# The first norm of a two-layer backbone: row-wise modulation in a block of its own, or tiles turned unscaled and modulated by feature inside the modulation's block

## The chip, the core and the metric

The kernel runs on one NeuronCore of one Trainium2 chip. Everything is one launch, and the metric is the device time of that launch in microseconds. All data are float32. The core's engines are TensorE (PE, with its weight loads PEld), VectorE (DVE), ScalarE (ACT), GpSimd (POOL) and the queues; SP only issues DMAs. Each engine runs its own program in order and waits on semaphores.

## What is computed

A diffusion backbone of two layers over 256 context tokens and 512 latent tokens, 1024 features each. Each layer normalises and modulates its input, mixes tokens by two kinds of attention or a gated linear scan, and then sends each token through 128 experts picked from 16384. The part that matters here is the very beginning of layer 0:

```python
def rmsnorm(x, g):
    y = x * lax.rsqrt(jnp.mean(x * x, axis=-1, keepdims=True) + EPS)
    return y * g

def modulate(h, shift, scale):
    return h * (1 + scale) + shift

def modulation(cvec, w_mod, b_mod):            # w_mod: (1024, 6 * 1024)
    m = jax.nn.silu(cvec) @ w_mod + b_mod
    return jnp.split(m, 6, axis=-1)

mx = modulation(c, w_mod[i], b_mod[i])         # latent stream
mc = modulation(c_ctx, w_mod[i], b_mod[i])     # context stream
hx = modulate(rmsnorm(x, norm1[i]), mx[0], mx[1])
hc = modulate(rmsnorm(h, norm1[i]), mc[0], mc[1])
ox, oc = mix_even(hx, hc, e_w_in[j], ...)      # begins with h @ w_in, w_in: (1024, 2304)
```

So for each of the two streams there is one shift and one scale vector of 1024 features, and the normed input is `x / rms(x) * gain * (1 + scale) + shift`. The gain times (1 + scale), and the shift, depend on the feature alone; 1 / rms depends on the token alone.

## The kernel before

Tokens lie on partitions in six tiles of 128 (`NT` = 6; tiles 0 and 1, `CT` = 2, are context, 2 to 5 are latent) in the SBUF tensor `R` (128 x 6 x 1024). A matmul against the 1024 features wants the features on partitions, so the normed tiles are turned by TensorE (a transpose is a matmul against the identity `ident`) into `hT` (128 x 8 x 768: feature within a block of 128, block `k` of `KC` = 8, token).

The program is a row of blocks (`nc.Block()`): in each, every engine gets its own list, and all engines meet at its end. The end of a block, together with the clearing of the semaphores of its stage on SP, is a barrier. The blocks at the start of the launch are these:

1. `start` (stage "mod", lines 183 to 252). SP loads `c` and `c_ctx`, then eight pieces of `w_mod` of 1 MB each (line 140), for columns 0 to 2047 of the modulation: shift and scale of the first norm. The ring `w` has eight places (`Modulation(m, a, s, 0, [0], KC, (0, 1))`). ACT computes an exponential for silu (line 205), and then issues all the other loads on its own queue: six small ones (lines 207 to 209), the band mask (210), `R` in two transfers of 1 and 2 MB (211, 212), `ident` (213), `iota` (214). PE multiplies each piece as it lands (line 159: four matmuls per piece, a stationary operand of two columns, one per stream, in four column groups of the array). DVE adds the bias (line 170, four instructions, into `row`: four groups of two partitions, at partitions 0, 32, 64, 96, 512 columns each). POOL stores these rows to the DRAM tensor `modulations` (line 178). ACT ends its list with a wait for all of its loads.
2. `modulated_norm` (stage "n00", lines 275 to 333). SP reads the gain and the four modulation rows back from DRAM, each spread over 128 partitions (lines 269, 272: `NormVectors.load`), and then prefetches the first two fifths of the projection's weights (line 359, four transfers of 1 MB). ACT takes the sum of squares of each tile (296) and a root (298). DVE makes gain * (1 + scale) for both streams (310), a reciprocal (315), and for each tile `R * (1/rms) * scale` (319) and `+ shift` (322). PE turns the tile (331, eight transposes of 128 x 128, two PSUM banks), ACT copies it to `hT` (302). Two pairs of PSUM banks alternate.
3. `project_heads` (stage "ph0", line 365 on). PE runs 30 units (`units`, line 430): 5 column blocks `n` by 6 tiles `t`, each of eight matmuls over `k` (shown as 16 by the trace), with `hT[:, k, t * P:(t + 1) * P]` as the stationary operand, into four PSUM banks. ACT squares a unit's result (445), DVE sums (475), scales and rotates it. DVE first waits for the tables of gains, cosines and sines (`tables_loaded`), which SP issues at the block's beginning (lines 410, 412). From unit 10 on, pieces of the modulation's later columns are slipped in between the units.

After that come the attention of the context, the experts of layer 0, layer 1 and its experts. The experts take most of the launch; they gather 8 KB rows of two tables from HBM.

## Time and profile before

| | us |
|---|---|
| three runs of the kernel before | 4306.64, 4318.24, 4319.30 |
| their median | 4318.24 |
| the profiled execution's own time | 4310.87 |
| its span, from first to last instruction | 4309.5 |
| blocks `start` and `modulated_norm`: start of the launch to the first matmul of the projection | 69.9 |

In the rows further down, times are microseconds from the start of the span, and a matmul of the program may be counted as two instructions. A row of the timeline gives the start, the length, the engine (PEld is TensorE's weight load; SPq, ACTq and DVEq are the instruction queues of these engines, where DMAs are issued), the line, the operation, output <- input, and how many instructions are merged in the row; in brackets stands the idle time of that engine ahead of it and what ended it. `PEclk` is the granted clock of TensorE as a share of 2.4 GHz.

### The profile page before, as it was taken

The numbers are of one execution on the slowest core, as the hardware profiler recorded it, in microseconds if no ns is written. First come the engines' busy times: TensorE is split into PE (matmuls) and PEld (weight loads), VectorE is DVE, ScalarE is ACT, GpSimd is POOL, SyncE is SP. The second block draws the span as 40 slices with busy tenths as digits, with TensorE's granted clock in tenths as the row PEclk, the third lists the DMA queues.
The fourth block names the chain that finished last, engine by engine and source line by source line (L and its number), as shares of the span: only waits on it lengthen the run. The fifth ranks groups of instructions, "written<-read, shape, count | busy, mean of one in ns | idle before, by whom it ended". The sixth has DMA issues, their size and how long they took to land. (4 is left out here: it accounts for less than half of the span.)

```text
span 4309.5 us, 44681 instructions
## 1 busy us (share of the span) xinstructions
PE 3738.7 (87%) x12806; PEld 1933.6 (45%) x12806; DVE 2605.5 (60%) x5677; ACT 1754.8 (41%) x5153; POOL 1700.3 (39%) x1349
## 2 busy tenths in 40 slices
PE   5998798899999899978898978788999997787877
PEld 2345644555554445423444436556444552222222
DVE  2534787667865855687654445437876458766544
ACT  1123355555554443433333334323663333333333
POOL 0100244444444444445444432002444435556665
PEclk9999999999999999999999999899999999999999
DMA  4354899999999999999999983028999999999998
GB/s 178 148 225 178 328 422 408 402 421 422 397 421 426 425 419 425 427 391 427 427 427 427 427 360 111 1 106 321 421 413 426 424 423 403 427 427 427 427 427 359
DMA packets 245901, 1561.98 MB, mean 362 GB/s; under 512 B 30995, under 2 KB 41267, under 8 KB 74518
## 3 DMA queue, kind: packets, MB, share of 16 engines
q0 software_dynamic: 185088, 1342.36, 74.5%
q1 hardware_dynamic: 56998, 211.95, 13.0%
q10 hardware_dynamic: 3568, 4.81, 0.3%
q8 instruction: 102, 1.67, 0.1%
q14 instruction: 145, 1.19, 0.1%
HBM read 1550.65 MB, written 8.36 MB: 362 GB/s over the span
## 5 line engine op out<-in xcount | busy, mean ns | idle before, releaser
L2898 PE MATMUL ps<-ring,ex_diag 128*128 128x512 f32 x5120 | 2474.1, 618 | 408.2 <-ACT ex_diag L2887 380.1
L1657 POOL DMA_INDIRECT ring<-in_p_uv,expert x1280 | 1643.9, 1284 | 2146.9 <-PE ps L2898 1417.1
L2862 DVE SCALAR_TENSOR_TENSOR ring<-ring,H 128x1024 f32<-128x1024 f32 x1280 | 1558.1, 1224 | 1085.4 <-DMA ring<-in_p_uv,expert 1059.9
L2898 PEld LDWEIGHTS ps<-ring,ex_diag 128*128 128x128 f32 x5120 | 924.7, 194 | 1644.7 <-ACT ex_diag L2887 819.5
L2881 ACT ACTIVATE ex_act_w<-ex_dots 128x1 f32<-128x1 f32 x1280 | 257.9, 201 | 1463.3 <-DVE ring L2862 1454.0
L2887 ACT ACTIVATE ex_diag<-ident_sb,ex_weight 128x128 f32<-128x128 f32 x1280 | 514.0, 402 | 93.0 <-issue 4.7
L2883 ACT ACTIVATE ex_weight<-ex_act_w,gates 128x1 f32<-128x1 f32 x1280 | 377.1, 295 | 90.8 <-issue 3.5
L430 PE MATMUL ps<-win_w,hT 128*128 128x512 f32 (+1 forms) x480 | 191.9, 557 | 1.6 <-PEq L283 1.4
L430 PEld LDWEIGHTS ps<-win_w,hT 128*128 128x128 f32 x480 | 90.4, 191 | 104.4 <-issue 102.1
L2020 PEld LDWEIGHTS ps<-hTc,bs_w 128*128 128x128 f32 x768 | 110.8, 191 | 29.3 <-issue 23.5
L2020 PE MATMUL ps<-hTc,bs_w 128*128 128x128 f32 (+1 forms) x768 | 120.3, 310 | 0.3 <-issue 0.3
L2862 DVE DVE_READ_ACCUMULATOR ring<-ring,H 128x1 f32 x1280 | 104.7, 82 | 0.0
L2881 ACT ACT_TABLE_LOAD x72 | 92.4, 1283 | 1.9 <-issue 0.3
L445 ACT ACTIVATE ph_sq<-ps 128x512 f32<-128x512 f32 (+1 forms) x24 | 12.4, 517 | 164.9 <-PE ps L430 164.9
L475 DVE TENSOR_REDUCE ph_ss<-ph_sq 128x8 f32<-128x512 f32 (+1 forms) x24 | 14.1, 585 | 100.3 <-ACT ph_sq L445 100.3
L664 PEld LDWEIGHTS ps<-KV,bs_probsT 128*128 128x128 f32 x480 | 63.1, 192 | 24.4 <-issue 24.4
L751 ACT COPY bs_probsT<-ps 128x512 f32<-128x512 f32 (+1 forms) x72 | 36.8, 511 | 84.2 <-PE ps L676 73.9
L735 DVE TENSOR_REDUCE bs_top<-ps 128x2 f32<-128x1536 f32 (+2 forms) x32 | 49.8, 1557 | 33.8 <-PE ps L688 32.4
L2165 PEld LDWEIGHTS ps<-bs_w,hTc 128*128 128x128 f32 x512 | 60.9, 192 | 11.5 <-issue 11.5
L2020 PE MATMUL ps<-K,bs_w 128*128 128x256 f32 x256 | 65.7, 379 | 0.0
L1813 ACT COPY fc_qT<-ps 128x128 f32<-128x128 f32 x64 | 17.0, 265 | 115.1 <-PE ps L1770 111.2
L664 PE MATMUL ps<-KV,bs_probsT 128*128 128x64 f32 (+1 forms) x480 | 63.2, 271 | 0.1
(478 smaller groups left out, 3392.1 us busy)
## 6 DMA issues: line engine op xcount, KB each, us to landing
bs_w<-in_p_wqk SPq DMA_DIRECT2D x64, 576.0 KB
ring<-in_p_wqk SPq DMA_DIRECT2D x48, 576.0 KB, 4.9
ca_mod_w<-in_w_mod SPq DMA_DIRECT2D x24, 1024.0 KB, 12.8
ring<-in_p_uv,expert POOLq DMA_INDIRECT x1280
win_mod_w<-in_w_mod SPq DMA_DIRECT2D x16, 1024.0 KB, 4.9
bs_w<-in_e_w_out_tiles SPq DMA_DIRECT2D x24, 512.0 KB
win_w<-in_e_w_in SPq DMA_DIRECT2D x9, 1024.0 KB, 10.0
fc_w_q<-in_p_wqk SPq DMA_DIRECT2D x16, 576.0 KB
```

The source lines that it names most:

```text
L430: mm = pe.matmul(m.ps[:, u % 4, 0:halves * 256], m.hT[:, k, t * P:(t + 1) * P], pre.w[:, n % 2, 0:halves, k, :], start=(k == 0), stop=(k = ...
L664: mm = pe.matmul(self.O[:, cols], self.probsT[:, r % 2, x * P:(x + 1) * P], KV[:, self.blocks(n)[j], vals], start=(j == 0), stop=(j == las ...
L735: dve.tensor_reduce(self.top[:, n % 2, :], self.S[:, :, 0:w], AX.X, ALU.max)
L751: act.copy(self.probsT[:, r % 2, 0:wide], self.T[:, 0:wide]).then_inc(self.copied, 1)
L1657: pool.indirect_dma_start(m.ring[:, r, :], None, a["p_uv"], bass.IndirectOffsetOnAxis(ap=m.expert[:, t % 2, slot % SLOTS:slot % SLOTS + 1] ...
L2020: mm = pe.matmul(m.ps[:, self.q_banks[u % nq], 0:cols], w[:, j * P:(j + 1) * P], self.turned_of(self.tiles_of(u), j), start=(j == 0), stop ...
L2165: mm = pe.matmul(m.ps[:, 7, at:at + P], self.hT[:, k, i * P:(i + 1) * P], w[:, k * P:(k + 1) * P], start=(k == 0), stop=(k == KC - 1), ski ...
L2862: dve.scalar_tensor_tensor(out=ring[:, r, 0:D], in0=ring[:, r, 0:D], scalar=1.0, in1=h_of(t + t0), op0=ALU.mult, op1=ALU.mult, accum_out=d ...
L2881: act.activation(act_w[:, b:b + 1], dots[:, t % 2, n:n + 1], ACT.Gelu)
L2883: act.activation(weight[:, b:b + 1], act_w[:, b:b + 1], ACT.Copy, scale=gates[:, t % 2, n:n + 1])
L2887: act.activation(diag[:, b, :], m.ident[:, :], ACT.Copy, scale=weight[:, b:b + 1]).then_inc(diag_ready, 1)
L2898: mm = pe.matmul(mix_banks(t)[:, half, :], diag[:, b, :], ring[:, r, D + half * BANK:D + (half + 1) * BANK], start=(n == 0), stop=(n == SL ...
```

## The change

`start` takes over the whole norm, and `modulated_norm` and `NormVectors` are gone, with the block they made.

- ACT issues the two transfers of `R` and `ident` first, ahead of the exponential for silu, and the small ones behind it, with one new one: the gain by feature (`norm1_features`, 128 x 8, the eight feature blocks of each partition), laid out on the host.
- ACT then waits for `R` and `ident`, squares the six tiles, takes the root; DVE multiplies each tile by 1/rms alone (`Hn`, tensor_scalar); PE turns the tiles, ACT copies them unmodulated to `hT`.
- The ring of `w_mod` pieces has four places in place of eight. On PE, tiles 0 to 3 are turned between and behind the last four pieces, tiles 4 and 5 at the end.
- The modulation rows no longer go to DRAM and back. PE turns them from `row` with sixteen transposes of two partitions into 128 x 2 columns each; DVE copies these from PSUM (`feature`) and makes `h_shift` and `h_scale` (128 x 8 x 2: feature, block, stream). A multiply and an add with one scalar per partition (`modulate`) then treat `hT` in place, eight instructions for a stream: the context's inside the block, the latent's at the beginning of `project_heads` on DVE, where PE waits for it (`latent_ready`) ahead of unit 2.
- SP issues the prefetch of the projection's weights behind the last piece of `w_mod`.
- `eps` is set at the beginning.

```diff
     with Stage(nc, "mod") as s:
...
-        mods = Modulation(m, a, s, 0, [0], KC, (0, 1))
+        mods = Modulation(m, a, s, 0, [0], 4, (0, 1))
...
             @block.sync
             def _(sp):
...
                 mods.sync(sp)
+                pre.prefetch(sp)
 
             @block.scalar
             def _(act):
+                act.dma_start(m.R[:, 0:CT, :], a["ctx"].rearrange("b (t p) d -> p (b t) d", p=P)).then_inc(tiles_loaded, 16)
+                act.dma_start(m.R[:, CT:NT, :], a["x"].rearrange("b (t p) d -> p (b t) d", p=P)).then_inc(tiles_loaded, 16)
+                act.dma_start(m.ident[:, :], a["ident"]).then_inc(tiles_loaded, 16)
                 act.wait_ge(c_loaded, 32)
                 act.activation(den[:, :, :], craw[:, :, :], ACT.Exp, scale=-1.0).then_inc(exp_done, 1)
+                act.dma_start(gain[:, :], a["norm1_features"]).then_inc(gain_loaded, 16)
...
                 act.dma_start(m.iota[:, :], rows(a["iota"])).then_inc(streams_loaded, 16)
+                act.wait_ge(tiles_loaded, 48)
+                act.wait_ge(eps_ready, 1)
+                for t in range(NT):
+                    act.activation(Hn[:, t, :], m.R[:, t, :], ACT.Square, accum_out=ss[:, t:t + 1])
+                    act.drain()
+                act.activation(ss[:, :], ss[:, :], ACT.Sqrt, bias=m.eps[:, :], scale=1.0 / D).then_inc(rms_ready, 1)
+                for t in range(NT):
+                    act.wait_ge(turned, t + 1)
+                    act.copy(m.hT[:, :, t * P:(t + 1) * P],
+                             m.ps[:, 2 + 2 * (t % 2):4 + 2 * (t % 2), :].rearrange("p b (k c) -> p (b k) c", c=P)).then_inc(copied, 1)
...
             @block.tensor
             def _(pe):
+                def turn(t):
+                    pe.wait_ge(h_ready, t + 1)
+                    if t >= 2:
+                        pe.wait_ge(copied, t - 1)
+                    for k in range(KC):
+                        tr = pe.transpose(m.ps[:, 2 + 2 * (t % 2) + k // 4, (k % 4) * P:(k % 4 + 1) * P],
+                                          Hn[:, t, k * P:(k + 1) * P], m.ident[:, :])
+                    tr.then_inc(turned, 1)
+
                 pe.wait_ge(silu_done, 1)
                 for n in range(mods.pieces):
                     mods.tensor(pe, n)
+                    if n >= mods.pieces - 4:
+                        turn(n - mods.pieces + 4)
+                for t in range(4, NT):
+                    turn(t)
+                pe.wait_ge(mods.row_ready, mods.COLS)
+                for n in range(ROWS):
+                    part, at = slice(32 * (n // 4), 32 * (n // 4) + 2), n % 4 * P
+                    tr = pe.transpose(m.ps[:, ROW_BANKS[n // 4], n % 4 * 2:n % 4 * 2 + 2], mods.row[part, 0, at:at + P], m.ident[part, part])
+                    if n % 4 == 3:
+                        tr.then_inc(rows_turned, 1)
...
                 dve.tensor_tensor(m.csil[:, :, 2:4].rearrange("p k s -> p s k"), craw[:, :, :], den[:, :, :],
                                   ALU.mult).then_inc(silu_done, 1)
+                dve.wait_ge(rms_ready, 1)
+                dve.reciprocal(ss[:, :], ss[:, :])
+                dve.drain()
+                for t in range(NT):
+                    dve.tensor_scalar(Hn[:, t, :], m.R[:, t, :], ss[:, t:t + 1], None, ALU.mult).then_inc(h_ready, 1)
                 mods.vector(dve, 0)
...
+                for j, bank in enumerate(ROW_BANKS):
+                    dve.wait_ge(rows_turned, j + 1)
+                    dve.tensor_copy(feature[:, 4 * j:4 * j + 4, :], m.ps[:, bank, 0:8].rearrange("p (n s) -> p n s", s=2))
+                dve.drain()
+                dve.wait_ge(gain_loaded, 16)
+                dve.tensor_copy(m.h_shift[:, :, :], feature[:, 0:KC, :])
+                dve.scalar_tensor_tensor(out=m.h_scale[:, :, :], in0=feature[:, KC:ROWS, :], scalar=1.0,
+                                         in1=gain[:, :].unsqueeze(2).broadcast_to([P, KC, 2]), op0=ALU.add, op1=ALU.mult)
+                dve.drain()
+                dve.wait_ge(copied, NT)
+                modulate(dve, m, 1)
                 dve.wait_ge(lam_exp_done, 1)
...
-            @block.gpsimd
-            def _(pool):
-                mods.store(pool)
...
+def modulate(dve, m, stream):
+
+    cols = slice(0, CT * P) if stream else slice(CT * P, TOK)
+    for k in range(KC):
+        done = dve.tensor_scalar(m.hT[:, k, cols], m.hT[:, k, cols], m.h_scale[:, k, stream:stream + 1],
+                                 m.h_shift[:, k, stream:stream + 1], ALU.mult, ALU.add)
+    return done
...
                     if t == 0:
                         pe.wait_ge(pre.loaded[n % 2], 16 * (2 * (n // 2) + halves))
+                    if u == CT:
+                        pe.wait_ge(latent_ready, 1)
...
+                modulate(dve, m, 0).then_inc(latent_ready, 1)
                 dve.wait_ge(tables_loaded, 96)
```

How the order moves on three engines. First TensorE, from the start of the launch, before (L159 the pieces of the modulation, L331 the turning of tiles, L430 the projection):

```order
L219 UNCONDITIONAL_BRANCH
L159 MATMUL ps<-mod_mod_w,csil 2x512 x32
L195 UNCONDITIONAL_BRANCH
L324 UNCONDITIONAL_BRANCH
L331 MATMUL ps<-ident_sb,Hn 128x128 x48
L283 UNCONDITIONAL_BRANCH
L421 UNCONDITIONAL_BRANCH
L430 MATMUL ps<-win_w,hT 128x512 x88
```

and TensorE now (L242 turns the tiles, L256 the modulation rows, L408 is the projection):

```order
L159 MATMUL ps<-mod_mod_w,csil 2x512 x20
L242 MATMUL ps<-ident_sb,Hn 128x128 x8
L159 MATMUL ps<-mod_mod_w,csil 2x512 x4
L242 MATMUL ps<-ident_sb,Hn 128x128 x8
L159 MATMUL ps<-mod_mod_w,csil 2x512 x4
L242 MATMUL ps<-ident_sb,Hn 128x128 x8
L159 MATMUL ps<-mod_mod_w,csil 2x512 x4
L242 MATMUL ps<-ident_sb,Hn 128x128 x24
L256 MATMUL ps<-ident_sb,mod_mod_row 128x2 x16
L199 UNCONDITIONAL_BRANCH
L397 UNCONDITIONAL_BRANCH
L408 MATMUL ps<-win_w,hT 128x512 x88
```

The turning has moved in between the pieces, so that pieces 5 to 7 stand behind the turning of tiles 0 to 2; one pair of branches (the end of a block) is gone.

Next ScalarE's queue at the start of the launch, before:

```order
L205 ACTIVATE mod_den<-mod_craw 128x16
L207 DMA mod_v<-in_a_lq 128x64
...
L208 DMA sink<-in_b_sink 128x8
L209 DMA gain_gn<-in_a_gn 128x128
L210 DMA band_sb<-in_band 128x2x128
L211 DMA R<-in_ctx 128x2x1024
L212 DMA R<-in_x 128x4x1024
L213 DMA ident_sb<-in_ident 128x128
L214 DMA iota_sb<-in_iota 128x16
```

and now:

```order
L209 DMA R<-in_ctx 128x2x1024
L210 DMA R<-in_x 128x4x1024
L211 DMA ident_sb<-in_ident 128x128
L213 ACT_TABLE_LOAD
L213 ACTIVATE mod_den<-mod_craw 128x16
L214 DMA mod_gain<-in_norm_features 128x8
...
L219 DMA band_sb<-in_band 128x2x128
L220 DMA iota_sb<-in_iota 128x16
L224 ACTIVATE Hn,mod_ss<-R 128x1024 x6
L226 ACT_TABLE_LOAD
L226 ACTIVATE mod_ss<-mod_ss,eps 128x6
```

The large transfers are now first on the queue, and the squares stand behind nine further issues on the same engine.

Last VectorE, behind silu, now (L275 is the multiply by 1/rms, L306 the modulation by feature; before, L319 and L322 stood here for each tile, in the second block):

```order
L272 RECIPROCAL mod_ss<-mod_ss 128x6
L275 TENSOR_SCALAR Hn<-R,mod_ss 128x1024 x6
L170 TENSOR_TENSOR mod_mod_row<-ps,mod_mod_bias 2x512 x4
...
L287 COPY mod_feature<-ps 128x8 x4
L290 COPY h_shift<-mod_feature 128x16
L291 SCALAR_TENSOR_TENSOR h_scale<-mod_feature,mod_gain 128x16
L306 TENSOR_SCALAR hT<-hT,h_scale,h_shift 128x256 x8
L298 SCALAR_TENSOR_TENSOR neg_lam<-mod_dots 128x1
L199 UNCONDITIONAL_BRANCH
L447 UNCONDITIONAL_BRANCH
L306 TENSOR_SCALAR hT<-hT,h_scale,h_shift 128x512 x8
```

The bias of the modulation (L170) stands behind the six multiplies, and behind it stands the chain that now ends the block.

## Rows read from the trace of the kernel before

**Rows 1.** Timeline of the first block, 0 to 36 us, all engines.
```profile
3.08 0.22 ACT L205 ACTIVATE mod_den<-mod_craw 128x16 f32<-128x16 f32 x1 [1.06 <-DMA mod_craw<-in_c_ctx]
...
4.96 0.45 ACTq L208 DMA_DIRECT2D sink<-in_b_sink  x1
5.45 1.32 ACTq L209 DMA_DIRECT2D gain_gn<-in_a_gn  x1
...
9.03 0.53 ACTq L212 DMA_DIRECT2D R<-in_x  x1
9.59 12.33 ACTq L213 DMA_DIRECT2D ident_sb<-in_ident  x1
...
21.95 2.31 ACTq L214 DMA_DIRECT2D iota_sb<-in_iota  x1
...
25.70 1.89 PE L159 MATMUL ps<-mod_mod_w,csil 128*2 128x512 f32 x8 [0.79 <-DMA mod_mod_w<-in_w_mod]
...
28.46 1.89 PE L159 MATMUL ps<-mod_mod_w,csil 128*2 128x512 f32 x8 [0.88 <-DMA mod_mod_w<-in_w_mod]
30.42 2.84 DVE L170 TENSOR_TENSOR mod_mod_row<-ps,mod_mod_bias 2x512 f32<-2x512 f32 x4 [26.32 <-PE ps L159]
```
**Rows 2.** Timeline of the second block, 36 to 70 us.
```profile
38.05 1.06 ACT L296 ACTIVATE Hn<-R 128x1024 f32<-128x1024 f32 x1 [3.79 <-PEq L195]
...
46.63 0.30 ACT L298 ACTIVATE n_ss<-n_ss,eps 128x6 f32<-128x6 f32 x1
49.60 2.36 DVE L310 SCALAR_TENSOR_TENSOR v_scale<-v_scale,v_gain 128x1024 f32<-128x1024 f32 x2 [15.15 <-DMA v_shift<-modulations]
52.08 0.19 DVE L315 RECIPROCAL n_ss<-n_ss 128x6 f32<-128x6 f32 x1
52.36 1.28 DVE L319 SCALAR_TENSOR_TENSOR Hn<-R,n_ss,v_scale 128x1024 f32<-128x1024 f32 x1
53.73 1.23 DVE L322 TENSOR_TENSOR Hn<-Hn,v_shift 128x1024 f32<-128x1024 f32 x1
...
55.01 1.97 PE L331 MATMUL ps<-ident_sb,Hn 128*128 128x128 f32 x8 [24.65 <-DVE Hn L322]
...
57.50 1.97 PE L331 MATMUL ps<-ident_sb,Hn 128*128 128x128 f32 x8 [0.53 <-DVE Hn L322]
...
67.48 1.09 PE L331 MATMUL ps<-ident_sb,Hn 128*128 128x128 f32 x8 [0.77 <-DVE Hn L322]
68.61 1.01 ACT L302 COPY hT<-ps 128x1024 f32<-128x1024 f32 x1 [0.85 <-PE ps L331]
```
**Rows 3.** Timeline, the projection's first work on each engine.
```profile
69.93 43.04 PE L430 MATMUL ps<-win_w,hT 128*128 128x512 f32 x96 [1.36 <-PEq L283]
...
72.56 0.51 SPq L412 DMA_DIRECT2D ph_sin<-in_rope_ab_sin  x1
...
78.67 0.60 ACT L445 ACTIVATE ph_sq<-ps 128x512 f32<-128x512 f32 x1 [9.05 <-PE ps L430]
...
85.54 0.60 ACT L445 ACTIVATE ph_sq<-ps 128x512 f32<-128x512 f32 x1 [6.27 <-PE ps L430]
```
**Rows 4.** Transfers issued from 0 to 120 us: count, size, us to landing.
```profile
R<-in_x ACTq DMA_DIRECT2D x1, 2048.0 KB, 25.6
...
gain_gn<-in_a_gn ACTq DMA_DIRECT2D x1, 64.0 KB, 18.9
...
ph_sin<-in_rope_ab_sin SPq DMA_DIRECT2D x1, 128.0 KB, 4.2
...
sink<-in_b_sink ACTq DMA_DIRECT2D x1, 4.0 KB, 16.7
```
**Rows 5.** Queues from 22 to 24 us: packets, MB, share; q1 is SP's, q10 ACT's.
```profile
DMA packets 213, 0.84 MB, mean 422 GB/s; under 512 B 19, under 2 KB 116, under 8 KB 116
...
q10 hardware_dynamic: 107, 0.05, 8.5%
q1 hardware_dynamic: 106, 0.79, 93.9%
```
**Rows 6.** The same from 26 to 28 us, where SP's pieces end.
```profile
q10 hardware_dynamic: 206, 0.57, 71.7%
q1 hardware_dynamic: 40, 0.22, 26.5%
```
**Rows 7.** TensorE's instructions of line 159, by tensor: min/median/max ns.
```profile
L159 PE MATMUL ps<-win_mod_w,csil x128: 589/592/592, 147.7 to 262.4; 128*2 128x512 f32 x128
...
L159 PE MATMUL ps<-mod_mod_w,csil x64: 1012/1036/1061, 6.8 to 29.3; 128*2 128x512 f32 x64
```
**Rows 8.** A warm group of line 159, and one of eight transposes, in the timeline.
```profile
155.94 1.04 PE L159 MATMUL ps<-win_mod_w,csil 128*2 128x512 f32 x8
...
411.41 1.04 PE L1759 MATMUL ps<-ident_sb,H 128*128 128x128 f32 x8
```
**Rows 9.** TensorE by stretch, 380 to 384 us: length, PE busy (instructions), PEclk, DMA share, GB/s.
```profile
380.00:381.00 1.00, 0.36 (x2) 0.50 0.98 356
381.00:382.00 1.00, 1.00 (x7) 0.50 1.04 414
382.00:383.00 1.00, 1.00 (x6) 0.50 0.86 270
383.00:384.00 1.00, 1.00 (x8) 0.61 0.96 365
```
**Rows 10.** The same by stretch, where the projection begins.
```profile
69.00:70.00 1.00, 0.07 (x1) 0.87 0.00 0
70.00:71.00 1.00, 1.00 (x2) 0.50 0.00 0
...
73.00:74.00 1.00, 1.00 (x3) 0.92 0.10 25
```
**Rows 11.** Groups by line and shape, VectorE: count, busy us, mean ns of one.
```profile
L720 DVE TENSOR_SCALAR bs_probs<-bs_probs,bs_rec 128x768 f32<-128x768 f32 x16 | 10.0, 624 | 0.0
...
L720 DVE TENSOR_SCALAR ca_probs<-ca_probs,ca_rec 128x256 f32<-128x256 f32 x8 | 2.8, 344 | 0.0
```
**Rows 12.** Timeline: eight matmuls with two moving columns, the nearest to the rows' turning.
```profile
2693.73 1.37 PE L1418 MATMUL ps<-lu_tri,LG 128*128 128x2 f32 x8
```

More of the change, by code:

```diff
@@ L180, in store, with start @@
             queue.wait_ge(self.stored[q], 16 * self.COLS * ((len(self.groups) - q + 1) // 2))
-def start(nc, m, a):
+def start(nc, m, a, pre, Hn):
+    ROWS, ROW_BANKS = 2 * KC, (6, 7, 0, 1)
     with Stage(nc, "mod") as s:
@@ L190, in start @@
         c_loaded, exp_done, silu_done = s.sem("c_loaded"), s.sem("exp_done"), s.sem("silu_done")
-        mods = Modulation(m, a, s, 0, [0], KC, (0, 1))
+        mods = Modulation(m, a, s, 0, [0], 4, (0, 1))
         v, junk, dots = s.sb("v", [P, 4, A_DQK]), s.sb("junk", [P, 2, A_DQK]), s.sb("dots", [P, 2])
-        v_loaded, streams_loaded = s.sem("v_loaded"), s.sem("streams_loaded")
-        dots_ready, lam_exp_done = s.sem("dots_ready"), s.sem("lam_exp_done")
+        ss, gain, feature = s.sb("ss", [P, NT]), s.sb("gain", [P, KC]), s.sb("feature", [P, ROWS, 2])
+        v_loaded, streams_loaded, tiles_loaded, gain_loaded = (s.sem(x) for x in ("v_loaded", "streams_loaded", "tiles_loaded", "gain_loaded"))
+        dots_ready, lam_exp_done, eps_ready = s.sem("dots_ready"), s.sem("lam_exp_done"), s.sem("eps_ready")
+        rms_ready, h_ready, turned, copied, rows_turned = (s.sem(x) for x in ("rms_ready", "h_ready", "turned", "copied", "rows_turned"))
         with nc.Block() as block:
@@ L227, in _ @@
                 dve.memset(m.csil[:, :, :], 0.0)
+                dve.memset(m.eps[:, :], EPS).then_inc(eps_ready, 1)
                 dve.wait_ge(exp_done, 1)
@@ L2956, in program @@
         CTILES, XTILES = range(CT), range(CT, NT)
-        m.h0 = 0
-        start(nc, m, a)
+        m.h_shift, m.h_scale = (ctx.enter_context(nc.sbuf_tensor(x, [P, KC, 2], F32)) for x in ("h_shift", "h_scale"))
         def later_scores(layer):
@@ L2962, in later_scores @@
             return both.rearrange("p t d -> p (t d)").rearrange("p (h k) -> p h k", k=NK)
+        m.h0 = 0
         m.later_scores = later_scores
@@ L2967, in program @@
             with nc.sbuf_tensor("hT0", [P, KC, TOK], F32) as m.hT:
-                with nc.sbuf_tensor("Hn", [P, NT, D], F32) as Hn, Stage(nc, "win0") as s:
-                    pre, mods = InWeights(m, a, s), Modulation(m, a, s, 0, [1, 2], 2, (4, 5))
-                    with Stage(nc, "v00") as sv:
-                        vec = NormVectors(m, a, sv, 0, 0, "norm1", (0, 1))
-                        def prefetch(sp):
-                            vec.load(sp)
-                            pre.prefetch(sp)
-                        modulated_norm(nc, m, "n00", vec, range(NT), lambda t: Hn[:, t, :], prefetch)
-                    project_heads(nc, m, a, pre, mods)
+                with Stage(nc, "win0") as s:
+                    pre = InWeights(m, a, s)
+                    with nc.sbuf_tensor("Hn", [P, NT, D], F32) as Hn:
+                        start(nc, m, a, pre, Hn)
+                    with Stage(nc, "win0m") as sm:
+                        project_heads(nc, m, a, pre, Modulation(m, a, sm, 0, [1, 2], 2, (4, 5)))
                 context_attention(nc, m, a)
```

75 lines of the change are left out of this document (3 added, 72 removed).

## The prediction

> **What bounds the kernel now.** The change touches only the launch's first 70 us, so I read the timeline of that stretch first, then the DMA queues by stretch, and last the clock of TensorE. Blocks are barriers, so each has its own bound.
>
> In the first block the bound is the loads. TensorE's last piece of the modulation begins at 28.46 and is over at 30.4; VectorE's bias is done at 33.3 [rows 1], and `R`, issued at 9.03 and landing 25.6 us later [rows 4], comes at 34.6. The second block starts at 38.05 (its first square), and there a chain runs that no engine fills: the modulation rows come back from DRAM, and VectorE waits 15.15 us for them, until 49.60; then scale rows (2.36), reciprocal, and per tile 1.28 + 1.23 us of VectorE, a new tile every 2.5 us; the first tile is turned at 55.01, the last at 67.48, the last copy ends at 69.62 [rows 2]. The projection's first matmul is at 69.93 [rows 3]. From there on TensorE works without gaps: one unit takes 6.87 us (85.54 - 78.67 [rows 3]). So whatever the start of the projection gains should reach the end, and nothing else in the launch is touched. The sum is therefore one question: when does the projection start, instead of at 69.93?
>
> **The change part by part.**
>
> (a) The trip through DRAM, one barrier and the second source of VectorE's work go. Gone are 12 instructions of about 1.25 us and the two of 2.36 us together on VectorE [rows 2], and the waits around them. Nothing of that is on the new path; what is late instead is worked out step by step.
>
> (b) When `R` is there. From the start ACT's queue and SP's share the 16 DMA engines. In rows 5 they moved 106 and 107 packets in the same 2 us, though in bytes 0.79 against 0.05 MB: the engines alternate packet by packet. SP's packets are 8 KB (0.79 MB / 106), those of `R` 4 KB (256 + 512 rows). A pair is then 12 KB, at 422 GB/s [rows 5] 29 ns, and 768 pairs take 22.4 us. Starting at about 2.6 (0.75 issue and the latency of the first loads), `R` is in at 25; `ident`, 128 short packets that alternate with 8 KB ones, adds 128 x 20 ns = 2.6: 27.6. Between SP's last packet (40 of them from 26 us on [rows 6], so about 26.9) and the matmul that waits for it at 28.46 [rows 1] lie 1.5 us. So ACT sees the tiles at about 29. Bounds: alone, `R`'s 3.1 MB at 422 GB/s take 7.5 us, which gives about 12; behind all of SP's pieces, as now, 34.6.
>
> (c) When ACT gets to them. Nine more issues stand between, and ACT stops while its queue is full: the issue of `ident` took 12.33 us, up to 21.92, and that of `iota` 2.31, up to 24.26 [rows 1]; these are the landing times of `sink` (4.96 + 16.7) and `gain_gn` (5.45 + 18.9) [rows 4]. In both cases what then remained ahead was of one size (`gain_gn`, the band, `R`; or the band, `R`, `ident`). In the new order the issue of `iota` is held in the same way until `ident` has landed, or the gain behind it, 2.9 us later (29 to 32). I take 30.3 for the first square, between the two; it lies above (b)'s 29, so a little of ACT's queue is on the path. The exponential for silu now stands behind three issues, which costs about 1 us, and TensorE then waits for the first piece anyway. If it were held as `ident` was before, the pieces would come later and `R` sooner, and TensorE would wait for `R` in both cases: no cost.
>
> (d) Squares and root: as before, 38.05 to 46.93 = 8.9 us [rows 2]. 39.2.
>
> (e) Reciprocal 0.19 and the gap behind it, 0.3 together [rows 2], then the first multiply. 128x768 takes 624 ns and 128x256 344 ns [rows 11], so 0.55 ns per element and 0.2 fixed: 0.77 for 1024. The first tile is ready at about 40.4, and one more every 0.77 us, faster than TensorE turns them.
>
> (f) TensorE from 40.4. Piece 4 is long done; queued behind the wait for tile 0 are pieces 5 to 7 (this is the wait that the change adds), then the turns. Nine groups follow: six turns and three pieces. Cold, a turn takes 1.97 [rows 2] and a piece 1.89 [rows 1]; warm 1.09 or 1.04 and 1.04 [rows 2, 8]. The same instruction takes 1036 against 592 ns [rows 7], which is the clock at 1.2 or 2.4 GHz. In rows 9 TensorE was at 0.50 from 380.6 on, turned tiles without a gap, and rose after 383; at the projection it ran without a gap from 69.93 and rose at about 73 [rows 10]. The nine groups stand without a gap too, so I take the first two cold (1.97, and 1.7 with the rise in it) and seven warm at 1.05: 11.0, with turns done at 51.4 and piece 7 at 48.3. The copies (1.01) keep up, two PSUM pairs being in turn. Upper bound, all cold: 6 x 1.97 + 3 x 1.89 = 17.5.
>
> The Trainium skill speaks against this ("TensorE: Matmul & The Clock Gate", Part 4: PE-mode transpose): it says that the full clock doesn't engage for instructions in transpose mode. Rows 9 disagree, since the granted clock rose while only transposes had run. By the page the sum would be that of rival 1.
>
> (g) VectorE behind piece 7: bias 2.84 [rows 1], 48.3 to 51.3, under the last turns. The small ones behind it (0.7) lie under the next step.
>
> (h) Sixteen transposes of rows. No row shows them. Nearest is L1418, with 8 in 1.37 [rows 12], 0.17 each; a full transpose is 0.13 warm and 0.25 cold (1.04 / 8, 1.97 / 8). Bounds 2.1 to 3.9; I take 2.3: 51.5 to 53.8.
>
> (i) VectorE: the last small copy, two small instructions and their drains, each about 0.2 like the reciprocal [rows 2]: 0.8, 54.6. Then eight multiplies of 128x256: 344 ns alone [rows 11], about 0.31 in a row: 2.5, bounds 2.0 to 2.8. With `neg_lam` 57.3. ACT's exponential with two table loads more lies beside this, and the second load (in the projection) is under 6.87 us of matmuls.
>
> (j) Barrier 0.3 (69.62 to 69.93 [rows 2, 3]): 57.6, less the rounding above: projection at **57.4**, instead of 69.93, **12.5 us** earlier.
>
> (k) Inside the projection: the latent modulation, 8 x 0.48 = 3.9 us (0.2 + 512 x 0.55 ns) on VectorE. Queued behind it is the first sum, needed 8.7 us in (78.67 - 69.93 [rows 3]), and PE needs its result after 15.6 us. Hidden with 4 us to spare. SP issues the tables later by the clearing of more semaphores (0.3 us); the last landed at 72.56 + 4.2 = 76.8 [rows 3, 4], 6.9 us in, against 9.3 for the sum: hidden with 2 us to spare. The weights (4 MB, 10 us) follow the pieces from about 33 on and are in by 45. The norm's own chain is their cover; without it they would cost their 10 us (4.2 MB at 422 GB/s).
>
> **Sum.** The profiled execution took 4310.87, 1.4 more than its span; less 12.5 gives 4298.4. It lies 7.4 us under the median of three runs (4318.24), which would give 4305.7. The four executions run from 4306.64 to 4319.30, with their middle at 4314.5; I take that as the level and forecast **4302**. The measurement tells about 0.3% (13 us) from no change, so the forecast lies just inside "no difference", at 0.29%.
>
> **The rivals.**
>
> 1. *TensorE stays cold through the turning.* For it: in the first block 1.89 of every 2.7 us were busy, and no group got faster [rows 1]; tiles turned from 55.01 with gaps of 0.53 were fast only at 67.48 [rows 2]. Against: there are no such gaps here, and rows 9. Then (f) is 17.5 and (h) 3.9, 8.1 more, of which none is covered: projection at 65.5, gain 4.4: 4310. Chance 0.18.
>
> 2. *ACT is sooner at the tiles.* If the queues don't share packet by packet from the start (only long-filled queues show it), or the issue isn't held, the squares begin at 24 to 28 and the gain is 15 to 19: about 4298. For it: ACT issues a microsecond ahead of SP. Against: rows 5. Chance 0.14.
>
> 3. *Slower: the projection runs on the half clock.* TensorE now waits some 3.6 us (53.8 to 57.4) for VectorE just ahead of the projection, where it waited 1.36 before [rows 3], and even then the clock was 0.50 until 73 [rows 10]. A unit at half clock costs 6.87 more. The gain is used up after 1.8 such units; 25.5 / 6.87 = 3.7 units make it slower by 13 us: 4328 with four. Against: both times the clock came back after some 3 us without gaps [rows 9, 10], and the projection has none. Chance 0.05.
>
> 4. *The gain is given back later*, in a stage bound by DMA or by the clock, so that nothing is left: 4314. For it: most of the launch is gather traffic. Against: all stages start behind one another, so an earlier start has nothing to collide with. Chance 0.05.
>
> **How the numbers follow.** The forecast's case has 0.58, with a gain of 8 to 17 by the bounds of (b), (c), (h) and (i). About 0.24 of it lies above 13 us, 0.34 below. Faster: 0.24 + 0.14 = 0.38. Same: 0.34 + 0.18 + 0.05 = 0.57. Slower: 0.05. For the range, gains of 1 to 19 on levels of 4308 to 4318 give 4289 to 4317; the slower case is left out.
>
> **What would show it.** `R` lands at 24 to 27 and `ident` 2 to 3 us behind; the first square is at 29 to 32 and the issue of `iota` is a long one. TensorE stands still from the end of piece 4 to about 40. Then nine groups follow without a gap, the first at 1.97, the last at 1.05. The first modulation by feature is at 54 to 55, the projection's first matmul at 56 to 59, and unit after unit comes 6.87 apart. Beyond it the trace should be the old one, shifted. It would be wrong if the first square came outside 27 to 34, if the turns stayed near 1.97, if the row transposes cost above 0.3 us each, or if TensorE waited in unit 2 for the latent part.

## The result, and the profile after

The changed kernel takes 4324.68 us (median of 15 runs, 4319.78 to 4332.37) against 4313.67 for the kernel before (15 runs, 4306.64 to 4321.41): a ratio of 1.0025, with a 95% interval of 1.0018 to 1.0032. It is slower by 11 us, where 12 us faster was forecast, and 4324.68 lies above the range (4289 to 4317). The profiled execution of the changed kernel has a span of 4330.0 us, 20.5 above that of before; it is one of the longer ones of its 15, so the two traces lie further apart than the medians do.

The stretch that the change is about went better than forecast. This is the timeline of the changed kernel's first block and of the start of the projection; the rows answer to [rows 1 to 3]:

```profile
2.32 1.28 ACT L213 ACT_TABLE_LOAD   x1 [2.32 <-issue]
3.71 19.57 SPq L140 DMA_DIRECT2D mod_mod_w<-in_w_mod  x7
5.91 0.22 ACT L213 ACTIVATE mod_den<-mod_craw 128x16 f32<-128x16 f32 x1 [2.30 <-DMA mod_craw<-in_c_ctx]
...
10.28 1.89 PE L159 MATMUL ps<-mod_mod_w,csil 128*2 128x512 f32 x8 [10.28 <-DMA mod_mod_w<-in_w_mod]
...
18.40 4.73 ACTq L220 DMA_DIRECT2D iota_sb<-in_iota  x1
...
23.24 1.06 ACT L224 ACTIVATE Hn<-R 128x1024 f32<-128x1024 f32 x1 [17.12 <-DMA ident_sb<-in_ident]
...
31.81 0.30 ACT L226 ACTIVATE mod_ss<-mod_ss,eps 128x6 f32<-128x6 f32 x1
...
32.42 4.07 DVE L275 TENSOR_SCALAR Hn<-R,mod_ss 128x1024 f32<-128x1024 f32 x6
...
33.22 1.97 PE L242 MATMUL ps<-ident_sb,Hn 128*128 128x128 f32 x8 [8.48 <-DVE Hn L275]
...
35.12 1.57 PE L159 MATMUL ps<-mod_mod_w,csil 128*2 128x512 f32 x8
...
36.63 1.10 PE L242 MATMUL ps<-ident_sb,Hn 128*128 128x128 f32 x8
...
40.76 2.84 DVE L170 TENSOR_TENSOR mod_mod_row<-ps,mod_mod_bias 2x512 f32<-2x512 f32 x4 [4.27 <-PE ps L159]
...
42.91 1.06 PE L242 MATMUL ps<-ident_sb,Hn 128*128 128x128 f32 x8 [0.32 <-ACT hT L229]
...
43.90 0.44 PE L256 MATMUL ps<-ident_sb,mod_mod_row 2*128 2x2 f32 x16
...
45.13 2.68 DVE L306 TENSOR_SCALAR hT<-hT,h_scale,h_shift 128x256 f32<-128x256 f32 x8
...
48.18 27.25 PE L408 MATMUL ps<-win_w,hT 128*128 128x512 f32 x57 [3.83 <-PEq L199]
48.18 3.74 DVE L306 TENSOR_SCALAR hT<-hT,h_scale,h_shift 128x512 f32<-128x512 f32 x8 [0.31 <-PEq L199]
```

The projection starts at 48.18, 21.75 us earlier than before (69.93, [rows 3]). Yet the launch ends 20.5 us later, so between these two traces 42 us were lost behind it. The issues of the experts' gathers say where. The gathers land in a ring of eight row buffers (`ring0` for layer 0, `ring1` for layer 1). In the answer by tile for this ring, each row is one layer: x768 and x512 gathers, min/median/max ns of an issue, then the first and the last start. First the kernel before:

```profile
L1657 POOL DMA_INDIRECT ring<-in_p_uv,expert x768: 936/942/2807, 484.0 to 2550.0; - x192
L1657 POOL DMA_INDIRECT ring<-in_p_uv,expert x512: 936/1344/2797, 2963.8 to 4281.3; - x171
```

and then the changed kernel:

```profile
L1636 POOL DMA_INDIRECT ring<-in_p_uv,expert x768: 932/939/3048, 469.6 to 2556.1; - x192
L1636 POOL DMA_INDIRECT ring<-in_p_uv,expert x512: 932/1378/2612, 2970.8 to 4301.6; - x171
```

The experts of layer 0 begin 14.4 us earlier and end 6.1 later: 2086.5 in place of 2066.0 us, 1.0% longer. Those of layer 1 take 1330.8 in place of 1317.5, again 1.0%. Together that is 33.8 us, in code that the change doesn't touch; 0.9 more lie between the two layers. The rest lies ahead: the attention of the context took 104.1 in place of 98.4 us (a part that differs from trace to trace, as shown further down). Together 33.8 + 0.9 + 5.7 and 1.8 in smaller pieces (the projection, the way to the first gather, the end) make the 42.

What is different in the experts is the rate of the transfers. Both layers have long stretches in which the 16 DMA engines are busy all the time. From 2100 to 2500 us the kernel before moved (packets, MB, mean rate; q0 are the gathers):

```profile
DMA packets 23887, 170.65 MB, mean 427 GB/s; under 512 B 2649, under 2 KB 2649, under 8 KB 4057
q0 software_dynamic: 22284, 162.30, 96.1%
```

and the changed kernel in the same stretch:

```profile
DMA packets 23614, 168.60 MB, mean 422 GB/s; under 512 B 2626, under 2 KB 2626, under 8 KB 4034
q0 software_dynamic: 22011, 160.25, 96.2%
```

At the same full load 1.2% fewer bytes went through. The engines' own work on the gathered rows is hardly slower: in layer 0 the mean VectorE instruction takes 1225 ns (1224 before) and the mean matmul 620 (617 before).

### The profile page after: what moved, and what is told of

Read it like the earlier page. It is cut to its first block and busy times, and to the rows that moved or that the text cites. A ratio compares the mean times of both kernels' runs of the same rounds, so it can differ in the third digit from the quotient of the medians.

```text
span 4330.0 us, 44703 instructions
## 1 busy us (share of the span) xinstructions
PE 3749.8 (87%) x12822; PEld 1936.1 (45%) x12822; DVE 2600.2 (60%) x5691; ACT 1756.9 (41%) x5155; POOL 1708.2 (39%) x1345
## 5 line engine op out<-in xcount | busy, mean ns | idle before, releaser
L2841 DVE SCALAR_TENSOR_TENSOR ring<-ring,H 128x1024 f32<-128x1024 f32 x1280 | 1558.3, 1225 | 1128.8 <-DMA ring<-in_p_uv,expert 1100.3
L408 PE MATMUL ps<-win_w,hT 128*128 128x512 f32 (+1 forms) x480 | 192.8, 559 | 4.1 <-PEq L199 3.8
L408 PEld LDWEIGHTS ps<-win_w,hT 128*128 128x128 f32 x480 | 90.6, 192 | 107.4 <-issue 105.1
## 6 DMA issues: line engine op xcount, KB each, us to landing
ca_mod_w<-in_w_mod SPq DMA_DIRECT2D x24, 1024.0 KB, 12.2
```

What stands on the lines that cost most here:

```text
L408: mm = pe.matmul(m.ps[:, u % 4, 0:halves * 256], m.hT[:, k, t * P:(t + 1) * P], pre.w[:, n % 2, 0:halves, k, :], start=(k == 0), stop=(k = ...
L2841: dve.scalar_tensor_tensor(out=ring[:, r, 0:D], in0=ring[:, r, 0:D], scalar=1.0, in1=h_of(t + t0), op0=ALU.mult, op1=ALU.mult, accum_out=d ...
```

## Which of four causes it is

Four things differ for the experts: the two new tensors `h_shift` and `h_scale`, 64 bytes of each partition each, stand behind the constants and move every later SBUF tensor by 128 bytes (theory A); the new input changes what lies where in HBM (theory B); the semaphores that the gathers use are numbered two lower, 186 to 193 in place of 188 to 195 (theory C); and everything starts earlier (theory D).

**e1** lets the two tensors live only where they are used:

```diff
-        m.h_shift, m.h_scale = (ctx.enter_context(nc.sbuf_tensor(x, [P, KC, 2], F32)) for x in ("h_shift", "h_scale"))
...
                     pre = InWeights(m, a, s)
+                    m.h_shift, m.h_scale = s.sb("h_shift", [P, KC, 2]), s.sb("h_scale", [P, KC, 2])
```

> The changed kernel with one edit: the two small tensors h_shift and h_scale (128 bytes of each partition together) live only in the stages that use them, so that every tensor behind them, the experts' rings among them, has its old SBUF address (ring0 at byte 108032 = 211 x 512 and ring1 at 110080 = 215 x 512, instead of 128 bytes further). Theory A (the 128 bytes shift the gathers' destinations off a 512-byte boundary, and this lowers the transfer rate from 427 to 421 GB/s): the two expert stages come back to 2066 and 1318 us, some 30 us less, and the whole gains about 14 to 20 us against the kernel before: 4294 to 4300. Theory B (place of the tables in HBM, by the new input), theory C (numbers of the semaphores, two lower now) and theory D (the earlier start meets another phase of clock or traffic): nothing changes here, 4325.

Measured: 4284.33 (6 runs, 4280.5 to 4294.46), a ratio of 0.9938 to the kernel before (0.9925 to 0.9950). The rest of the change is unaltered in it, with the input, the semaphores and the early start. So B, C and D are out as the main cause, and the change as written is worth a gain once these 128 bytes lie elsewhere, a larger one than the 14 to 20 us that theory A expected. The first and last gathers of e1:

```profile
L1636 POOL DMA_INDIRECT ring<-in_p_uv,expert x768: 935/941/3049, 465.6 to 2530.5; - x192
L1636 POOL DMA_INDIRECT ring<-in_p_uv,expert x512: 935/1452/2614, 2946.3 to 4265.7; - x171
```

2064.9 and 1319.4 us, as before (2066.0 and 1317.5). In its stretch from 2100 to 2500 us:

```profile
DMA packets 23887, 170.64 MB, mean 427 GB/s; under 512 B 2650, under 2 KB 2650, under 8 KB 4058
```

**e2** puts the shift alone into the kernel before:

```diff
         m.gain_gn = ctx.enter_context(nc.sbuf_tensor("gain_gn", [P, A_DV], F32))
+        m.pad = ctx.enter_context(nc.sbuf_tensor("pad", [P, 32], F32))
```

> The kernel before with one unused SBUF tensor of 128 bytes of each partition behind the constants, which shifts all later tensors by 128 bytes, and nothing else. Theory A: about 25 to 33 us slower than before, 4339 to 4347, with a plateau of 421 GB/s in the experts. Theories B, C and D: 4314, no change.

Measured: 4353.08 (5 runs), 1.0093 (1.0079 to 1.0107). An unused tensor costs 41 us, more than the 25 to 33 expected; the changed kernel against e1 shows about the same amount, 4324.68 - 4284.33 = 40 (38 by the two ratios). Its gathers take 2088.4 and 1331.0 us, 35.9 more than before, at the changed kernel's rate:

```profile
L1657 POOL DMA_INDIRECT ring<-in_p_uv,expert x768: 939/942/2697, 489.2 to 2577.6; - x192
L1657 POOL DMA_INDIRECT ring<-in_p_uv,expert x512: 939/1456/2974, 2992.4 to 4323.4; - x171
...
DMA packets 23617, 168.64 MB, mean 422 GB/s; under 512 B 2624, under 2 KB 2624, under 8 KB 4032
```

**e3** declares the new input in the kernel before and doesn't use it:

```diff
+    inputs["norm1_features"] = np.asarray(inputs["norm1"])[0].reshape(KC, P).T
     inputs["w_mod"] = inputs["w_mod"].reshape(L, P, KC, 3, 4 * BANK).transpose(0, 3, 2, 1, 4)
```

> The kernel before with the new input by feature (4 KB in HBM) declared and not used, so that the tensors in HBM are placed as in the changed kernel. Theory B: 25 to 33 us slower, about 4343. Theories A, C, D: no change, 4314.

Measured: 4310.52 (12 runs), 1.0002 (0.9993 to 1.0011). Theory B is out.

## What the shift must be, and of which tensor

**e4**, **e6** and **e10** are e2 with another size: `[P, 128]`, `[P, 64]` and `[P, 16]` in place of `[P, 32]`, that is 512, 256 and 64 bytes.

> The kernel before with an unused SBUF tensor of 512 bytes of each partition in the same place as in e2. Theory A: no change, 4314, since the rings stay on a 512-byte boundary. A theory by which any shift of the SBUF tensors costs (their place to one another is the same in all of these) would give 4339 to 4347, as for 128 bytes.

> As e2 with 256 bytes in place of 128. If the transfer needs a 512-byte boundary, it is as slow as e2, 4353 and 422 GB/s. If a multiple of 256 does, 4312 and 427 GB/s.

> As e2 with 64 bytes in place of 128. If only multiples of 256 bytes are fast and all others cost the same: 4350, 422 GB/s in the experts. If the cost goes with the part of a row that lies in a broken piece, between 4312 and 4350; if 64 bytes break more pieces than 128 do, above 4350.

| unused bytes | start of ring0 | us (median) | ratio, 95% interval | gathers, layer 0 and 1, us | MB from 2100 to 2500 us |
|---|---|---|---|---|---|
| 0 (before) | 108032 = 422 x 256 | 4313.67 | | 2066.0, 1317.5 | 170.65 |
| 64 (e10) | 108096 | 4352.99 | 1.0096 (1.0081 to 1.0111) | 2085.6, 1332.4 | 168.59 |
| 128 (e2) | 108160 | 4353.08 | 1.0093 (1.0079 to 1.0107) | 2088.4, 1331.0 | 168.64 |
| 256 (e6) | 108288 = 423 x 256 | 4313.88 | 1.0001 (0.9992 to 1.0010) | 2062.3, 1317.4 | 170.67 |
| 512 (e4) | 108544 = 424 x 256 | 4316.04 | 1.0006 (0.9997 to 1.0016) | 2063.8, 1318.0 | 170.67 |

My boundary of 512 bytes was too strict: e6 shows that a multiple of 256 is enough. And the cost is all or nothing, the same at 64 and at 128 bytes. The row of e10 in the same stretch:

```profile
DMA packets 23607, 168.59 MB, mean 421 GB/s; under 512 B 2620, under 2 KB 2620, under 8 KB 4028
```

The Trainium skill ("DMA: Bandwidth & Descriptors", How a descriptor splits into AXI transactions) has a rule with this threshold: for a descriptor that doesn't start at a multiple of 256 bytes, the first transaction starts at the boundary below its start, and the bytes ahead of the start cost beats too. The page words it for bytes that are fetched; here it is the destination in SBUF that was shifted. The threshold agrees with the runs. The size agrees less: by the page's count of beats an 8 KB row costs 260 in place of 256 at 128 bytes (an estimate, 1.6%) and 258 (0.8%) at 64, while the runs show 1.2% for both. So what the 256 bytes are in the hardware stays open; what the runs show is the threshold and the price.

**e5** shifts the rings and what is allocated behind them, and nothing ahead:

```diff
-            with nc.sbuf_tensor("hTc", [P, KC, CT * P], F32) as m.hT, nc.sbuf_tensor("ring0", [P, 8, 2 * D], F32) as m.ring:
+            with nc.sbuf_tensor("hTc", [P, KC, CT * P], F32) as m.hT, nc.sbuf_tensor("pad0", [P, 32], F32), nc.sbuf_tensor("ring0", [P, 8, 2 * D], F32) as m.ring:
...
-                with nc.sbuf_tensor("ring1", [P, 8, 2 * D], F32) as m.ring:
+                with nc.sbuf_tensor("pad1", [P, 32], F32), nc.sbuf_tensor("ring1", [P, 8, 2 * D], F32) as m.ring:
```

> The kernel before with 128 unused bytes of each partition just ahead of each of the two rings of the experts, so that the first block, the projection and the attention of the context keep their addresses. Theory A in its narrow form (the gathers' destinations alone carry the cost): as e2, 4353, about 40 us slower than before, with 422 GB/s in the experts. If the many other transfers and operands that e2 shifted too carry a share, less: between 4312 and 4353.

Measured: 4348.43 (5 runs), 1.0085 (1.0072 to 1.0099). The gathers take 2085.0 and 1332.5 us. **e7** is the counterpart: the changed kernel with `[P, 96]` in the same two places, so that only the rings (and what follows them) are back on the boundary, and everything ahead stays 128 bytes off.

> The changed kernel as it is, h_shift and h_scale in their place, with 384 more unused bytes ahead of each ring, so that the rings begin on a 512-byte boundary again (at 108544 and 110592) while the tensors ahead of them stay 128 bytes off. Narrow theory A: 4284, as e1. If the shift costs in the stages ahead too (the attention of the context took 5.8 us longer in the changed kernel), 4288 to 4292.

Measured: 4289.90 (5 runs), 0.9943 (0.9929 to 0.9956), with 2062.7 and 1318.0 us. Together: the shift costs where the rings are off (4348.43 - 4312.73, the kernel before beside it, is 36 us), and the shift of all that lies ahead costs nothing that can be measured (e5 lies within e2's interval, e7 within e1's). What stands behind the rings was moved with them in both, so the rings are named by their share of the bytes (162 of 171 MB in the stretch above), not by a run that moves them alone.

The 5.7 us that the attention of the context took longer in the changed kernel go neither with the addresses nor with the change. From its first transpose to the square behind it, it takes 96.7 to 104.3 us in the 13 traces (before, the changed kernel, e1 to e11), and the length roughly follows the mean granted clock in it: 96.7 at 0.93 (e6), 98.4 at 0.88 (before), 99.0 at 0.86 (e1), 99.5 at 0.88 (e11), 102.1 at 0.85 (e3 and e5), 104.1 to 104.3 at 0.83 (the changed kernel, e7, e9). e1 and e11 have the change and are short; e3 doesn't and is longer. The seven traces with the same addresses there (before, e1, e3, e5, e8, e9, e11) run from 98.4 to 104.2. So these 5.7 us are a difference between executions, and what makes TensorE fall to the lower level sooner in one than in another is open. Rows by stretch (length, busy time and instructions of PE, PEld, DVE, ACT, POOL, then PEclk, DMA share, GB/s), before and after:

```profile
290.00:300.00 10.00, 9.63 (x46) 3.51 (x45) 3.53 (x10) 2.62 (x10) 0.00 (x0) 0.75 1.02 429
340.00:350.00 10.00, 9.94 (x62) 4.87 (x62) 3.47 (x14) 4.51 (x16) 0.00 (x0) 0.86 0.05 20
```

```profile
270.00:280.00 10.00, 9.63 (x35) 3.08 (x38) 2.47 (x8) 1.68 (x7) 0.00 (x0) 0.57 1.01 424
320.00:330.00 10.00, 9.94 (x40) 4.49 (x39) 1.73 (x7) 2.46 (x8) 0.81 (x2) 0.51 0.08 30
```

## The start of the launch

With the shift out of the way, e1 shows what the change itself is worth. **e11** is e1 a second time.

> The kernel of e1 a second time, for its size: its projection starts 20.3 us earlier than before in the trace, and it measured 28 us (0.9938, 0.9925 to 0.9950). If the start is all, 0.9953 (4292); if some 8 us more come from what the earlier start meets later, 0.9935.

Measured: 4288.78 (5 runs), 0.9949 (0.9935 to 0.9962). The two together give 0.9938 and 0.9949, 22 to 27 us; the projection starts at 49.66 and 48.53 in their traces, 20.3 and 21.4 earlier than before. So nearly all of it is the start, and 1 to 6 us are not accounted for; they are no larger than the intervals.

The 1.1 us between the two starts is the clock. Both traces turn their first tile at 33.3. In e11 the second turn is fast already (1.09), as in the changed kernel; in e1 it isn't:

```profile
33.27 1.97 PE L242 MATMUL ps<-ident_sb,Hn 128*128 128x128 f32 x8 [7.62 <-DVE Hn L275]
...
36.98 1.97 PE L242 MATMUL ps<-ident_sb,Hn 128*128 128x128 f32 x8
...
40.10 1.10 PE L242 MATMUL ps<-ident_sb,Hn 128*128 128x128 f32 x8
```

The forecast had the projection at 57.4, and 48.18 came. 7.1 of the 9.2 us between lie at the first square, expected at 30.3 and seen at 23.24. `R` had landed early:

```profile
R<-in_x ACTq DMA_DIRECT2D x1, 2048.0 KB, 18.5
...
ident_sb<-in_ident ACTq DMA_DIRECT2D x1, 64.0 KB, 20.6
```

(1.25 + 18.5 = 19.8 and 1.76 + 20.6 = 22.4 us). The queues by stretch in the changed kernel, 0 to 5 and 8 to 12 us:

```profile
q10 hardware_dynamic: 249, 1.02, 60.3%
q1 hardware_dynamic: 144, 0.00, 1.4%
...
q1 hardware_dynamic: 150, 0.98, 60.0%
q10 hardware_dynamic: 152, 0.62, 39.5%
```

From 8 us on the queues alternate packet by packet, as the prediction had it. But in the first 5 us ACT's queue moved 1 MB of `R`, and SP's only short packets; `c` landed at 5.9 in place of 3.1, and the first piece of `w_mod`, behind it on SP's queue, was there for TensorE only at 10.28 in place of 6.82. **e9** takes this head start away by moving `R` and `ident` behind the exponential in e1:

```diff
-                act.dma_start(m.R[:, 0:CT, :], a["ctx"].rearrange("b (t p) d -> p (b t) d", p=P)).then_inc(tiles_loaded, 16)
-                act.dma_start(m.R[:, CT:NT, :], a["x"].rearrange("b (t p) d -> p (b t) d", p=P)).then_inc(tiles_loaded, 16)
-                act.dma_start(m.ident[:, :], a["ident"]).then_inc(tiles_loaded, 16)
                 act.wait_ge(c_loaded, 32)
                 act.activation(den[:, :, :], craw[:, :, :], ACT.Exp, scale=-1.0).then_inc(exp_done, 1)
+                (the same three lines)
```

> e1 with R and ident issued behind the exponential for silu on ACT's queue, as late as about 3.3 us in place of 0.75. The prediction let R share the DMA engines packet by packet from the beginning and had it at 25; it landed at 19.8. Theory E (R had a head start: in the first 5 us it moved 1.02 MB, while SP's two small loads of c stood between its packets and landed at 5.9 in place of 3.1): without the head start c is back at 3.1 and the first piece at about 7, R lands at 25 to 26, the first square comes at 27 to 29 and the projection starts at 53 to 55, 4 us later than in e1: 4288. Theory F (R came early since the ring of four pieces left the queue of SP empty): R still lands some 19 us behind its issue, at 22, with the projection at 51 to 52.

Measured: 4301.30 (7 runs), 0.9965 (0.9954 to 0.9976). Its timeline and landings:

```profile
3.10 0.21 ACT L210 ACTIVATE mod_den<-mod_craw 128x16 f32<-128x16 f32 x1 [1.08 <-DMA mod_craw<-in_c_ctx]
...
3.59 0.48 ACTq L212 DMA_DIRECT2D R<-in_x  x1
...
6.68 1.89 PE L159 MATMUL ps<-mod_mod_w,csil 128*2 128x512 f32 x8 [6.68 <-DMA mod_mod_w<-in_w_mod]
...
27.68 4.72 ACTq L220 DMA_DIRECT2D iota_sb<-in_iota  x1
32.51 1.06 ACT L224 ACTIVATE Hn<-R 128x1024 f32<-128x1024 f32 x1 [29.19 <-DMA ident_sb<-in_ident]
...
R<-in_x ACTq DMA_DIRECT2D x1, 2048.0 KB, 25.1
```

`R` is issued 2.3 us later and lands 8.9 us later (3.59 + 25.1 = 28.7), and the projection starts at 57.46, 7.8 us behind e1. That is the direction of theory E and twice its size; F, by which `R` would have landed at 22, is out, and in e9 as in the changed kernel the packets of both queues are equal once both are full. In the first 5 us of e9, ACT's queue moved nothing and SP's this:

```profile
DMA packets 378, 0.75 MB, mean 149 GB/s; under 512 B 288, under 2 KB 288, under 8 KB 288
...
q1 hardware_dynamic: 378, 0.75, 45.9%
```

288 short packets and the first 90 long ones were through before `R` moved. In the changed kernel only 144 of the short ones were through by then, and `R` moved beside them. The 144 took 1.4% of the engines' time there, beside 60.3% for the 249 packets of `R`. So I read the head start as this: `R` lost little time while SP's short packets passed beside it. No run moves the short packets alone. In e9 the first piece runs at 6.68; the second comes at 12.74 and the next three 3.9 us apart. That e9 starts its projection where the prediction had it (57.4) is chance: `R` landed at 28.7 in place of 25 and the first square came at 32.51 in place of 30.3, and the cheaper turning of the rows took most of this back. By its median e9 is 17 us behind e1 and 12.5 behind e11; the start explains 8 to 9 of these, and the attention of the context 5 in the traces (104.2 against 99.0 and 99.5).

**e8** asks what stands between `R` and the squares. In e1 these are two things: the issue of `iota`, held for 4.7 us until 23.2, and the landing of `ident` at 22.5 (1.77 + 20.7), which ACT waits for together with `R`. e8 takes away both; `ident` gets a semaphore of its own there (`ident_loaded`), for which TensorE waits ahead of the first turn:

```diff
-                act.dma_start(m.gain_gn[:, :], rows(a["a_gn"])).then_inc(v_loaded, 16)
-                act.dma_start(m.band[:, :, :], a["band"].rearrange("s p k -> p s k")).then_inc(streams_loaded, 16)
-                act.dma_start(m.iota[:, :], rows(a["iota"])).then_inc(streams_loaded, 16)
-                act.wait_ge(tiles_loaded, 48)
+                act.wait_ge(tiles_loaded, 32)
...
                 act.activation(ss[:, :], ss[:, :], ACT.Sqrt, bias=m.eps[:, :], scale=1.0 / D).then_inc(rms_ready, 1)
+                (the three issues)
...
+                    if n == mods.pieces - 4:
+                        pe.wait_ge(ident_loaded, 16)
```

> e1 with another order on ACT's queue: the gain, the four vectors and the sinks are issued as before, gain_gn, the band and iota only behind the root, and the squares wait for R alone, the turning for ident. In e1 the first square stood behind the issue of iota, which was held for 4.7 us until 23.2, while R had landed at 19.8. If the held issues are on the path, the first square comes at 19.8 to 20.5 and the projection starts 2.8 to 3.4 us earlier than in e1, at about 46.5: 4281. If TensorE's clock or the late landing of the band takes it back, the projection starts at 49 to 50 and the time is e1's.

Measured: 4281.86 (5 runs), 0.9930 (0.9916 to 0.9943). Its timeline:

```profile
19.66 1.06 ACT L222 ACTIVATE Hn<-R 128x1024 f32<-128x1024 f32 x1 [13.50 <-DMA R<-in_x]
...
27.86 0.49 ACTq L227 DMA_DIRECT2D iota_sb<-in_iota  x1
...
41.10 0.22 DVE L282 SCALAR_TENSOR_TENSOR mod_junk<-mod_v 128x64 f32<-128x64 f32 x1 [0.81 <-DMA gain_gn<-in_a_gn]
...
45.64 9.81 PE L411 MATMUL ps<-win_w,hT 128*128 128x512 f32 x17 [4.59 <-PEq L200]
```

The first square is at 19.66, right behind `R` and 3.6 us earlier than in e1 and e11, and the issues are no longer held. The projection starts at 45.64, 4.0 earlier than in e1 and 2.9 earlier than in e11; 0.8 us go back where VectorE waits for `gain_gn`, which is now issued late. e8 doesn't say how the 3.6 us divide. From e1's landings I estimate that moving the issues alone would have gained 0.7 us, since `ident` was there only at 22.5; the other 2.9 need the squares, which don't use `ident`, to stop waiting for it. By its median e8 is the fastest kernel here, though its interval overlaps those of e1 and e11. It beats both the kernel before and the changed one.

## Why the prediction was wrong

Its first part, on what bounds the kernel, ends with "nothing else in the launch is touched". **That is the step that failed.** I read "touched" off the instructions, which are the same beyond the projection, and not off the addresses. The line of the change that allocates `h_shift` and `h_scale` for the whole launch (the diff ahead of the prediction doesn't show it; e1 above takes it out) moves the destination of all 1280 gathers off a multiple of 256 bytes. The price of that alone is 41 us in e2, 39 in e10 and 36 in e5; the gain without it is 22 to 27 (e1 and e11). Both signs of the result hang on it: the mechanism that I worked out is real, and is covered by one that I didn't list. Rival 4 comes nearest ("a stage bound by DMA"), but its reason was another, it had the gain just used up, and I argued against it that an earlier start has nothing to collide with. The slower case (rival 3, the half clock) isn't what happened: the projection began at the lower clock as before, its first unit took 9.69 us in place of 8.74, and from its end on, up to 120 us, the granted clock was 1.00. That the result is slower, as rival 3 said, is no credit to it.

At the start of the launch the case that came is rival 2, to which I gave 0.14: ACT is sooner at the tiles, since `R` had a lead on SP's pieces. It went beyond even that case. The first square at 23.24 lies below its 24 to 28, and below the 27 that I had named as a sign of being wrong; the gain of 21.75 us lies above its 15 to 19. Had nothing else been touched, e1 and e11 say that the time would have been 4284 to 4289, at or just below the lower end of my range.

Step by step, on the start of the launch:

- (a) and (j), a barrier and the trip through DRAM gone: right. The end of the block costs 0.3.
- (b) the alternation of the queues: right in its kind (152 and 150 packets), wrong in what lay ahead of it. I let both start together; `R` was at 19.8, not 25. In e9, where SP's pieces are ahead, the later pieces come 3.9 us apart; 128 pairs of 29 ns each would give 3.7 (an estimate from [rows 5]).
- (c) the held issue: right. `iota`'s issue took 4.73 us and ended at 23.13, 0.8 after `ident` had landed (22.4), and the first square follows at once. I had put 1.3 on it. What I didn't ask is whether the squares need `ident` at all; e8 gains 3.6 us at the first square by dropping both waits.
- The exponential behind three issues: I expected 1 us and it was 2.8, since the loads of `c` shared with `R`. That it costs nothing is right; TensorE was through with piece 4 at 24.7 and waited for the first tile until 33.22.
- (d) 8.9 for squares and root: 8.87. (e) 1.2 to the first tile: 1.1, with six multiplies in 4.07, 0.68 each in place of 0.77.
- (f) nine groups in 11.0: 10.75 (33.22 to 43.97), the first at 1.97, the second at 1.57, then 1.04 to 1.10. The closeness is partly luck: e1, with the same instructions, needed 12.2 for the nine (33.27 to 45.45), because the clock rose later. Rival 1, by which the turning would have stayed cold, is out. The Trainium skill ("TensorE: Matmul & The Clock Gate", Part 4: PE-mode transpose) says that the full clock doesn't engage for transposes; here pieces stand between the turns, so this stretch doesn't test it. The kernel before does, and speaks against it: between 55.01 and 68.6 TensorE ran turns and nothing else, and the sixth took 1.09 in place of 1.97 [rows 2].
- (g) 2.84: right. (h) sixteen row transposes in 2.3, with bounds of 2.1 to 3.9: 0.44. The row I took as nearest [rows 12] gave a price five times too high. Its matmuls load weights of 128 rows and these load two, which may be why; no run isolates it.
- (i) 3.5 for the small ones and the modulation: 0.8 and 2.68. (k) 3.74 for the latent part, hidden; the tables too.

So the start's sum was too high by 9.2 us, 7.1 of it in (b) and (c) and 1.9 in (h), and the whole's sum lacked a term of 40 us with the other sign.

## What to carry to other kernels

An allocation is a change to everything that is allocated after it. Before a small persistent tensor is added, work out the new address of every buffer that bulk transfers land in. Here a start 64 or 128 bytes off a multiple of 256 took 1.2% of the rate in a stretch that DMA bounds, and 1.0% of the experts' time, while a tensor that lives only where it is needed (e1), or a shift of a whole 256 bytes (e6), cost nothing. The kernels here still have such a buffer: by its place in the list of allocations `R` begins at byte 16512, 128 off, in all of them, and no run moved it. When a change moves the time in stages it doesn't touch, compare the rates at full load first: 427 against 422 GB/s in a flat stretch told more than any wait.

On queues that share the DMA engines, what is issued first and alone can get a head start out of proportion to its lead (2.3 us of issue time were worth 8.9 us at the landing). An engine can stand still in an issue (ACT for 7.01 and 4.73 us in the changed kernel), and a wait for more than one needs holds it as well; work that is due belongs ahead of the issues that aren't and should wait for its own data alone (e8).
